# A two-layer diffusion backbone on one core: tile stores on ScalarE's queue, lower expert rows gathered earlier, one modulation chunk moved behind the gathers

## The reference

```python
def grouped_moe(h, router_w, router_bias, w_gate, w_up, w_down):
    ...
    for e in range(N_EXPERTS):
        y = (jax.nn.silu(h @ w_gate[e]) * (h @ w_up[e])) @ w_down[e]
        out = out + gates[:, e:e + 1].astype(h.dtype) * y
    return out
```

## Time and profile before

| what | value |
|---|---|
| median of 3 runs | 963.18 us (962.91 to 963.35) |
| profiled execution, its own time | 966.61 us |
| its span | 962.6 us |
| TensorE (PE) busy | 806.8 us, 84% |
| VectorE (DVE) busy | 450.0 us, 47% |
| ScalarE (ACT) busy | 265.1 us, 28% |
| GpSimd (POOL) busy | 188.3 us, 20% |
| DMA | 312.42 MB, mean 325 GB/s |
| chain that ended last | DMA 51%, PE 25%, DVE 18%, issue 3%, the rest below 3% each |

### The profile page before, as it was taken

One profiled execution on the slowest core, in us unless ns is written; L12 is line 12 of the kernel. 1 busy time (PEld: TensorE's weight loads), 2 busy tenths in 40 slices (PEclk: granted clock), 3 DMA queues, 4 the chain that ended last, 5 costly groups with the idle time before them and its releaser, 6 DMA issues.

```text
span 962.6 us, 31597 instructions
## 1 busy us (share of the span) xinstructions
PE 806.8 (84%) x13340; PEld 538.5 (56%) x13341; DVE 450.0 (47%) x1101; ACT 265.1 (28%) x464; POOL 188.3 (20%) x364
## 2 busy tenths in 40 slices
PE   3899999899969898989888549999968885586985
PEld 2444444444457676778666435458436764464763
DVE  2379999943574343444433261765263221121222
ACT  2313436331413231322222130255032220121222
POOL 2300000010043332343323400000005220111220
PEclk9999999999979998999999969999998997788998
DMA  9992397578479999999999992881666999999992
GB/s 347 352 383 97 141 378 291 176 261 305 166 310 378 407 407 410 412 413 413 414 418 406 388 343 85 303 324 51 262 257 243 416 407 424 422 427 420 426 419 80
DMA packets 70692, 312.42 MB, mean 325 GB/s; under 512 B 8972, under 2 KB 9376, under 8 KB 54256
## 3 DMA queue, kind: packets, MB, share of 16 engines
q1 hardware_dynamic: 54608, 275.78, 72.6%
q0 software_dynamic: 15040, 33.62, 9.5%
q10 hardware_dynamic: 992, 2.26, 0.6%
HBM read 297.38 MB, written 14.20 MB: 324 GB/s over the span
## 4 chain that ended last, share of the span: by engine, by line
DMA 51%; PE 25%; DVE 18%; issue 3%; SPq 2%; ACT 2%; POOL 0%; DVEq 0%; POOLq 0%; ACTq 0%
DMA weight_ring<-in_exp_w_down 11%; DMA weight_ring<-in_exp_w_up 10%; DMA weight_ring<-in_exp_w_gate 10%; DVE arena L1068 9%; PE ps L608 7%; DMA arena<-in_exp_w_up 7%; DMA hT<-in_exp_w_down 5%; DMA arena<-in_exp_w_gate 4%; PE ps L831 3%; PE ps L874 3%; DMA weight_ring<-in_ev_w_in 2%; PE ps L574 2%; SPq L370 2%; PE ps L914 1%; PE ps L775 1%
## 5 line engine op out<-in xcount | busy, mean ns | idle before, releaser
L775 PE MATMUL ps<-weight_ring,arena 128*32 128x128 f32 x5760 | 183.0, 290 | 45.5 <-DMA weight_ring<-in_exp_w_up 27.9
L775 PEld LDWEIGHTS ps<-weight_ring,arena 128*32 128x32 f32 x5760 | 173.4, 118 | 60.0 <-issue 27.1
L1373 DVE TENSOR_TENSOR arena<-arena,ps 128x64 f32<-128x64 f32 x128 | 28.3, 221 | 225.9 <-ACT arena L1757 222.8
L1757 ACT ACTIVATE arena<-ps 128x64 f32<-128x64 f32 x128 | 28.7, 224 | 364.6 <-PE ps L775 364.6
L574 PE MATMUL ps<-hT,weight_ring 128*128 128x512 f32 x256 | 114.7, 604 | 2.8 <-DMA weight_ring<-in_ev_w_in 2.5
L785 PE MATMUL ps<-weight_ring,arena 128*32 128x256 f32 x1440 | 92.4, 382 | 6.6 <-DMA weight_ring<-in_exp_w_down 4.2
L1068 DVE SCALAR_TENSOR_TENSOR arena<-arena,par 128x512 f32<-128x512 f32 x132 | 94.9, 750 | 4.0 <-DVE arena L1099 0.8
L775 PE MATMUL ps<-arena 128*32 128x128 f32 x2432 | 74.3, 281 | 19.0 <-DMA arena<-in_exp_w_up 17.0
L574 PEld LDWEIGHTS ps<-hT,weight_ring 128*128 128x128 f32 x256 | 48.2, 192 | 67.3 <-issue 63.1
L775 PEld LDWEIGHTS ps<-arena 128*32 128x32 f32 x2432 | 70.8, 114 | 24.2 <-issue 22.6
L1757 ACT ACT_TABLE_LOAD x64 | 82.1, 1283 | 6.6 <-DVEq L1332 1.5
(11 more groups left out here) (323 smaller groups left out, 868.9 us busy)
## 6 DMA issues: line engine op xcount, KB each, us to landing
weight_ring<-in_ada_w SPq DMA_DIRECT2D x24, 2048.0 KB, 14.2
weight_ring<-in_exp_w_gate SPq DMA_DIRECT2D x22, 2048.0 KB, 10.4
weight_ring<-in_exp_w_up SPq DMA_DIRECT2D x22, 2048.0 KB, 10.8
weight_ring<-in_exp_w_down SPq DMA_DIRECT2D x22, 2048.0 KB, 11.1
arena<-in_exp_w_gate SPq DMA_DIRECT2D x10, 2048.0 KB
hT<-in_exp_w_down SPq DMA_DIRECT2D x10, 2048.0 KB, 11.1
arena<-in_exp_w_up SPq DMA_DIRECT2D x10, 2048.0 KB
weight_ring<-in_ev_w_in SPq DMA_DIRECT2D x4, 2048.0 KB, 19.9
```

Of the source, the lines that this page charges most:

```text
L775: last = mm(ps[32 * qd:32 * qd + 32, 1 + hh, 0:P].rearrange("p (m n) -> p m n", m=2), xgT[:, MT * k:MT * k + MT], w2[:, k, :, at:at + 64], ...
L1757: s.activation(act_sl[:, 64 * hh:64 * hh + 64], ps[:, 1 + hh, 0:64], ACT.Silu).then_inc(s_sl[l], 1)
```

## The change

The 40 tile stores of layer 0 leave GpSimd's program and go to ScalarE's. ScalarE's loop now takes four tiles per trip: ahead of the Silus of tile k it waits for the output of tile k-1, stores it, waits until the store of tile k-4 has landed, and frees that buffer. TensorE adds to `s_gu` behind the last tile so that the last trip can run out. GpSimd's loop keeps the gathers alone and reaches `expert_rows` without having issued a store. `GAP_ADA` goes from 3 to 2: the third chunk of `ada_w` is loaded behind the wait for the upper rows, its product goes behind the fourth tile of the key/value product, in bank 5, and the slots and the order of use are written anew for it.

```diff
--- before.py
+++ after.py
@@ -64,8 +64,8 @@
        [("out0", 0, 0)] + _ada(0, 10, 12) + _ada(1, 0, 4) + [("out0", 0, 1)] + _ada(1, 4, 6))
 PRE_SLOT = [3, 4, 5, 2, 0, 1, 2, 3, 4, 5, 3, 4, 5, 3, 0, 1, 2, 4, 3, 1, 5, 2, 4, 3]
-GAP_ADA = 3
-MID = (_ada(1, 6, 9) + [("qkv", 0, 2), ("qkv", 0, 0)] + _ada(1, 9, 10) +
+GAP_ADA = 2
+MID = (_ada(1, 6, 8) + [("qkv", 0, 2), ("qkv", 0, 0)] + _ada(1, 8, 10) +
        [("qkv", 0, 1), ("out1", 0, 0), ("out1", 0, 1)] + _ada(1, 10, 12))
 PRE_COUNT = [PRE_SLOT[:i + 1].count(slot) for i, slot in enumerate(PRE_SLOT)]
@@ -85,8 +85,8 @@
 CONV_FIRST = {2: 2, 5: 2, 8: 2, 11: 2}
 CONV_AT = {1: 9, 2: 8, 3: 13, 4: 11, 5: 3, 6: 6, 7: 12, 8: 3, 9: 6, 10: 12, 11: 3, 12: 8, 13: 10, 14: 10}
-USE = [0, 1, 2, 3, 5, 4] + list(range(6, len(MID)))
-MID_SLOT = [3, 4, 5, 0, 2, 1, 3, 0, 1, 4, 5]
+USE = [0, 1, 2, 4, 5, 3] + list(range(6, len(MID)))
+MID_SLOT = [3, 4, 0, 2, 5, 1, 3, 0, 1, 4, 5]
 ROUND = float(3 * 2 ** 22)
@@ -814,6 +814,9 @@
                     pe.wait_ge(s_y[l], end + 1)
                     pe.wait_ge(s_spr, end + 1)
                     combine_tile()
+                else:
+                    pe.wait_ge(s_gu[l], end * 2 + 1)
+                    pe.sem_inc(s_gu[l], 2 * (AHEAD - 1))
                 for i in range(3 * SETS):
                     seen[i] += moe_n[i]
@@ -834,8 +837,8 @@
                     half_transposes(1)
                 if t == 1:
                     half_ready(KD - 1, 1)
-                if t == 2:
-                    ada_product(7)
+                if t >= CT:
+                    ada_product((7, 5)[t - CT])
             pe.wait_ge(s_qkv, NT)
             pe.sem_inc(used[slot], 1)
             def transpose_heads(un):
@@ -858,8 +861,6 @@
             for un in range(4):
                 c, i = un // 2, un % 2
                 if un == 1:
-                    pe.wait_ge(s_red, state["ada"] - 1)
-                if un == 3:
                     pe.wait_ge(s_red, state["ada"])
                 if i == 0:
                     slot = next_chunk()
@@ -1434,8 +1435,8 @@
             for t in range(NT):
                 dve.wait_ge(s_qkv, t + 1)
                 v.tensor_copy(kv[:, t, :], ps[:, t, :]).then_inc(s_qkve, 1)
-                if t == 2:
-                    read_columns(7)
+                if t >= CT:
+                    read_columns((7, 5)[t - CT])
             link(add_bias(1, 6, 10))
             link(gain(mods[:, 1, 8 * SC2:8 * SC2 + 8, :], 1, SC2, C_FFNG + 8))
             dve.sem_inc(s_mods, 1)
@@ -1751,11 +1752,38 @@
                 act.wait_ge(s_rt[l], 1)
                 total = act.value_load(ctl[0:1, 2, E - 1:E], min_val=E, max_val=MAXTILES)
-                with act.Fori(0, total) as g:
+                def silus(g):
                     for hh in range(2):
                         act.wait_ge(s_gu[l], g * 2 + (hh + 2))
                         s.activation(act_sl[:, 64 * hh:64 * hh + 64], ps[:, 1 + hh, 0:64], ACT.Silu).then_inc(s_sl[l], 1)
-                return total
+
+                if l:
+                    with act.Fori(0, total) as g:
+                        silus(g)
+                    return total
+
+                places = y_dram.rearrange("(g s) (q n) -> g q s n", s=MT, q=4)
+
+                def store(k, u):
+                    act.wait_ge(s_y[0], k + 2)
+                    act.dma_start(places[k], y_sb[u]).then_inc(s_yo[u], 16)
+
+                def four_tiles(j):
+
+                    for u in range(AHEAD):
+                        k = j * AHEAD + u
+                        if u or not isinstance(j, int):
+                            store(k - 1, (u - 1) % AHEAD)
+                        if not isinstance(j, int):
+                            act.wait_ge(s_yo[u], j * 16)
+                            act.sem_inc(s_yfree, 1)
+                        silus(k)
+
+                four_tiles(0)
+                rounds = (total + (AHEAD - 1)) >> 2
+                with act.Fori(1, rounds) as j:
+                    four_tiles(j)
+                store(rounds * AHEAD - 1, AHEAD - 1)
             router(0)
             moe(0)
@@ -1955,7 +1983,6 @@
                 pool.wait_ge(s_rt[l], 1)
                 pool.wait_ge(s_hst[l], 16 * n)
                 rows = h_dram[l].rearrange("t (q n) -> (t q) n", q=4)
-                places = y_dram.rearrange("(g s) (q n) -> g q s n", s=MT, q=4)
                 def gather(u, at):
@@ -2003,13 +2030,6 @@
                             pool.wait_ge(s_spr, k + 1)
                             pool.sem_inc(s_pool, 1)
                             g.tensor_copy(slot_cur[:, :], slot_tab[:, k, :]).then_inc(s_cur, 1)
-                        else:
-                            pool.wait_ge(s_y[0], k + 2)
-                            pool.sem_inc(s_pool, 1)
-                            g.dma_start(places[k], y_sb[u]).then_inc(s_yo[u], 16)
-                            if not isinstance(j, int) or nxt == 0:
-                                pool.wait_ge(s_yo[nxt], (j + (trips - 1)) * 16)
-                                pool.sem_inc(s_yfree, 1)
                 four_tiles(0)
                 with pool.Fori(1, (total + (AHEAD - 1)) >> 2) as j:
@@ -2019,8 +2039,6 @@
                     expert_rows(total)
                 for u in range(AHEAD):
                     pool.wait_ge(s_xgs[u], gathered(u, rounds + (1 if u else 2)))
-                    if not l:
-                        pool.wait_ge(s_yo[u], rounds * 16)
                 pool.sem_inc(s_pool, 1)
                 return rounds
```

## The result

The kernel after the change takes 1026.01 us (median of 6 runs, 1023.03 to 1029.67), the kernel before, beside it on the same chip, 963.04 (6 runs, 962.21 to 964.08). The ratio is 1.0652, 95% interval 1.0630 to 1.0674: slower by 63 us. The profiled execution took 1028.14 us, its span is 1026.4, which is 63.8 more than the 962.6 of before.

A forecast was written before the change was run, and what follows sets the result against it. The prediction took DMA to bound the experts' stage, then the gather seam, then TensorE. It summed 42.2-3.0+1.9-0.3=+40.8 onto 966.6 for 1007.4, less 3.4 for the median: 1004.0 us, range 954 to 1020.

The forecast's parts named there:

- part 1: First layer's experts: tile stores move from GpSimd's software queue to ScalarE's hardware queue; claimed to cost 42.2 us.
- A store with the outermost count 4 should use 4 of the 16 engines on this queue: Tile stores on ScalarE's queue: engines per copy are the largest divisor up to 16 of its outermost count, here 4.
- The same four always: Tile stores on ScalarE's queue: every store was assumed to land on the same four DMA engines.
- The first rival: Tile stores: the four engines change per store, or all share it, so part 1 is free; 958.3 us, chance 0.24.
- 38 x 1.11 = 42.2 us: Experts' stage: 38 stores each add 1.11 us to four engines (1.48 instead of 0.37), lengthening the stage by 42.2 us.
- the stage goes at the pace of the four: Experts' stage: each weight load uses all 16 engines and lands with the slowest, so the four engines set the pace.
- The price from above, 57: Upper bound of the 42.2 us: stores landing after 20.5 us make ScalarE wait, up to 15 us more, 57.
- ScalarE's wait holds TensorE: Experts' stage: stores on four engines land after over 18 us, holding tile k; some 15 us on top, 1019, chance 0.10.
- An engine with work in any queue loses nothing, only the order changes: Experts' stage: the argument against extra loss from queues taking turns, given against "ScalarE's wait holds TensorE".
- ScalarE's issue and table loads: ScalarE's loop: a store issue of 0.34 us fits in 0.99 free; table loads cost nothing, 13 us at worst.
- Parts 2 and 3: Seam after the experts: earlier lower gathers and a 2.10 MB chunk moved behind them; -3.0 seam, +1.9 product, -0.3 VectorE.
- The likeliest case: Whole kernel: the same four engines carry every store; 1004.0 us, own range 985 to 1020, chance 0.61.

The follow-up runs named there:

- quarters: The changed kernel with each tile store cut into four copies of 32 rows, outermost count 32, so 16 engines each; 959.61 us, 0.9960 of the kernel before.
- change_again: The changed kernel itself, run again beside other runs on one chip; 1022.75 us, 1.0629 of the kernel before.
- quarters_third: The same kernel as quarters, run again on one chip beside change_again; 959.97 us, 0.9961 of the kernel before.
- sync_four_apart: quarters plus a 128 KB copy on four engines ahead of each of 39 weight loads, on SyncE's queue, target quarters apart in DRAM; 1032.78 us, 1.0683 of before.
- halves: The changed kernel with each tile store cut by columns into two copies of 512 B pieces, both still on four engines; 1047.43 us, 1.0827 of before.
- eight_buffers: The changed kernel with 8 output buffers instead of 4, so ScalarE waits for the store of tile k-8; 1014.97 us, 1.0534 of before.
- sync_spread_again: quarters plus a 128 KB copy on 16 engines ahead of each of 39 weight loads, on SyncE's queue; 972.67 us, 1.0067 of before.

## Why the prediction was right or wrong

**The sign and the mechanism of part 1: right.** "A store with the outermost count 4 should use 4 of the 16 engines on this queue": 5280 packets more, as forecast, and with quarters the loss is gone. "The same four always": the share of 0.27 with several stores queued. The Trainium skill, DMA: Bandwidth & Descriptors, section Why a DMA increments its semaphore by 16 and not by 1, says that the engines of a hardware queue are the lowest-numbered ones of the core's 16; which numbers they have no run here shows, that they don't change the share does. The first rival (all or changing engines, 958.3) needed the opposite, and its figure is near what quarters did on two chips, 959.6 and 960.0; on the third it took 971.7.

**The failed step is the size of one term: "38 x 1.11 = 42.2 us", taken as "the term of the engines' own work" and nothing for waiting.** The four engines cost 62.8 us side by side (change_again less quarters_third). From 290 us to the last output the queues of the kernel after are these:

```profile
q1 hardware_dynamic: 9884, 91.69, 72.1%
q0 software_dynamic: 1974, 5.47, 5.2%
q10 hardware_dynamic: 5148, 5.11, 4.7%
```

If queues 1 and 0 are spread over all 16 engines and queue 10 lies on four, each of the four had (0.721+0.052+4 x 0.047) x 317 = 305 us of work up to the last output. Before it was (0.892+0.115) x 251 = 253. So of 66 us some 52 are more work on the four, and the other 14 or so are not: the four, too, rested for some 12 us (317-305), and before they had no rest at all.

The 52 are what the term meant, and it had them at 42.2: 39 stores took 59.6 us of each of the four, 1.53 and not 1.48; GpSimd's queue gave up 12.4 us for them, 0.32 a store and not 0.37; and the weights, of the same 91.7 MB, took 229 us and not 224. The 14 were put at nothing, because "the stage goes at the pace of the four" had them busy throughout. In their place the trace has SyncE waiting 105 us for TensorE instead of 15, and the DMA share of 0.00 at 576. How much of that is ScalarE's wait, and how much TensorE's lower granted clock (0.88, before 0.96), no run parts. For sync_four_apart the same account doesn't close: the recorded times of the packets on the four engines add up to 340 us in a stage of 323. So its 60.1 us, 1.54 per copy, stay undivided.

With the stage longer by 66 us, not 42, the same bytes gave 343 GB/s where "about 350" was forecast, and the last output came at 607, not 583. Put at 63 instead of 42.2, with all else as it was, the sum gives 1025; 1026 was measured. The price from above, 57, was 6 short. A cost per piece, 15 ns by halves, does not come on top: the 1.53 us are 48 ns for each of 32 pieces, and hold it.

**"ScalarE's wait holds TensorE" (0.10, +15): not excluded.** What it describes is in the trace: turns by the piece (18 us for a store beside weights; the forecast worked out 20.5), Silus up to 10.0 us behind their products, which the forecast itself had named as this rival's sign, and some 14 us beyond the engines' work where it asked for 15. Its figure, 1019, was the nearest of all, with a chance of 0.10. Against it stands sync_four_apart, where the whole of such a loss comes without the wait, and eight_buffers, which relieved the wait in part and gained 9 to 11 us, not all of it. So the wait is not needed for the loss, and what it carries of this one stays open. "An engine with work in any queue loses nothing, only the order changes" left out that the four run out of work when the loads come late.

**ScalarE's issue and table loads: right that they cost nothing.** The issue took 0.55 us, not 0.34, and the table loads at the Silus fell from 64 to 25. quarters has the same 25 and four issues per tile, at a share of 1.00 and without a loss.

**Parts 2 and 3: near in sum.** Forecast -3.0+1.9-0.3 = -1.4 us; the profile has -4.4 ahead of the key/value product and +1.3 from there on, -3.1. The lower gathers did start ahead of the last output. But the undoing of either part moved no time by more than can be told, so the seam's 3 us are a reading of single executions.

**The range.** 1020 was the top, 1026 came. It held 57 as the load's upper end, with 0.10 for more. The likeliest case was too narrow on its upper side: its bounds came from rows where no four engines were ever loaded unevenly.

## What to carry to other kernels

Before a store moves to a hardware queue, read its target's outermost count, and after it count the completions in the queue's packets: 4 of 16 engines cost 63 us of 963 here, and cutting the copy by its outermost dimension gave it back (0.996 to 1.005 of before). A few overloaded engines appear in the trace as waits of whichever engine sits behind the queue, so put the same load on another queue before calling that wait the cause, and compare the form of the two losses, not only the size. Compare variants that differ by 1% only side by side on one chip.

## What the runs showed of the hardware that was not expected

- Beside weight pieces of 16 KB a hardware queue of small pieces moves 7 per us on its four engines, with pieces of 1 KB (42 packets in 6 us) and of 512 B (44 in 6 us, halves) alike; alone it moves 96 GB/s.
- An issue on ScalarE blocks the engine when earlier copies are still queued: 7.6 us at worst with four buffers (8.0 in change_again), 23.0 with eight, where the median is 0.55.
- A target of 4 x 32 rows that lie end to end counts as one block and gets 16 engines; the same shape with gaps gets 4 (5616 and 5148 packets for 39 copies). The Trainium skill, in the section named above, says that the count goes by the pattern's dimension "as the instruction carries it"; these two runs agree with that.
- TensorE's granted clock fell from 0.96 to 0.88 in the experts' stage as its idle stretches grew; in the windows at 378 us it is 0.50, the lower of its two levels (1.2 GHz), while TensorE is busy all the time, after stretches in which it had stood. sync_four_apart has 0.92 there and sync_spread_again 0.97.
